# A delta-rule recurrence: rows kept in PSUM banks, and 16-wide diagonal blocks inverted elementwise on VectorE

## The reference

```
def step(state, inp):
    r_t, w_t, k_t, v_t, aa_t, bb_t = inp
    sa = jnp.einsum('bhvk,bhk->bhv', state, aa_t)
    state = state * w_t[:, :, None, :] + sa[..., None] * bb_t[:, :, None, :] + v_t[..., None] * k_t[:, :, None, :]
    return state, jnp.einsum('bhvk,bhk->bhv', state, r_t)
...
_, y = lax.scan(step, state0, (tm(r_h), tm(w_h), tm(k_h), tm(v_h), tm(-kk), tm(kk * a_h)))
```

## Time and profile before

| | us |
|---|---|
| median of three runs | 2084.86 (2081.75 to 2087.80) |
| the profiled execution, its own time | 2081.08 |
| its span in the trace | 2079.3 |
| TensorE busy | 2031.4 (98%) |
| VectorE busy | 1139.5 (55%) |
| GpSimd busy | 1178.7 (57%) |
| ScalarE busy | 536.0 (26%) |
| the recurrence, from the opening's D (1126.4) to the end of chain 6 (1565.9) | 439.5 |
| from one pair to the next in its middle | 61.4 |

### The profile page before, as it was taken

The page is one execution under the profiler, slowest core; times in us unless marked ns, Lnnn a source line. Parts: engine busy times, 40 slices in busy tenths (PEclk is TensorE's granted clock), DMA queues, the critical chain, the costliest instruction groups (busy, mean ns, idle before and its releaser), DMA issues.

```text
span 2079.3 us, 39898 instructions
## 1 busy us (share of the span) xinstructions
PE 2031.4 (98%) x16195; PEld 1678.5 (81%) x16195; DVE 1139.5 (55%) x1533; ACT 536.0 (26%) x1139; POOL 1178.7 (57%) x1175
## 2 busy tenths in 40 slices
PE   8999999999999999999999999999999999999998
PEld 6888888877877787788877888888886888888886
DVE  6878624466667654202068677666773655555312
ACT  2100002233434212313143133333223023333101
POOL 6888865634534475545547044433374867677764
PEclk9999999999999999999999999999999999999999
DMA  3323331353353422311323022111223432332231
GB/s 136 102 92 102 101 101 46 92 176 121 127 163 112 148 82 64 98 62 61 124 56 93 15 65 66 46 48 46 65 65 124 133 101 81 101 99 90 89 112 56
DMA packets 181243, 190.28 MB, mean 92 GB/s; under 512 B 8526, under 2 KB 162269, under 8 KB 180829
## 3 DMA queue, kind: packets, MB, share of 16 engines
q1 hardware_dynamic: 172288, 181.81, 27.6%
q10 hardware_dynamic: 8796, 6.21, 1.0%
HBM read 179.56 MB, written 8.44 MB: 90 GB/s over the span
## 4 chain that ended last, share of the span: by engine, by line
PE 61%; DVE 3%; issue 1%; POOL 1%; DVEq 1%; POOLq 1%; ACT 0%; ACTq 0%
PE bank L915 8%; PE bank L916 8%; PE bank L917 8%; PE bank L1592 7%; PE bank L1553 3%; PE bank L1405 3%; PE bank L1421 2%; PE bank L1423 2%; PE bank L1422 2%; PE bank L1690 2%; PE bank L1327 1%; PE bank L1328 1%; PE bank L1329 1%; PE bank L1080 1%; PE bank L1294 1%
## 5 line engine op out<-in xcount | busy, mean ns | idle before, releaser
L740 POOL TENSOR_SCALAR whi<-raws 128x1024 fp32r<-128x1024 f32 (+5 forms) x312 | 321.0, 1029 | 284.9 <-PE bank L1082 166.8
L746 POOL TENSOR_TENSOR wlo<-raws,whi 128x512 fp32r<-128x512 f32 (+5 forms) x312 | 400.8, 1285 | 0.0
L745 POOL TENSOR_TENSOR wlo<-raws,whi 128x512 fp32r<-128x512 f32 (+5 forms) x312 | 373.4, 1197 | 46.0 <-issue 3.0
L915 PE MATMUL bank<-hbuf,whi 128*128 128x512 f32 (+2 forms) x840 | 329.4, 392 | 1.8 <-POOL wlo L746 1.8
L917 PE MATMUL bank<-hbuf,wlo 128*128 128x512 f32 (+2 forms) x840 | 327.8, 390 | 0.0
L916 PE MATMUL bank<-hbuf,whi 128*128 128x512 f32 (+2 forms) x776 | 303.0, 390 | 0.0
L649 POOL TENSOR_TENSOR spare<-ones 1x1 f32<-1x1 f32 x92 | 21.4, 233 | 298.5 <-PE bank L917 208.2
L915 PEld LDWEIGHTS bank<-hbuf,whi 128*128 128x128 f32 (+2 forms) x840 | 157.1, 187 | 37.0 <-POOL wlo L746 3.1
L917 PEld LDWEIGHTS bank<-hbuf,wlo 128*128 128x128 f32 (+2 forms) x840 | 157.1, 187 | 34.1
L916 PEld LDWEIGHTS bank<-hbuf,whi 128*128 128x128 f32 (+2 forms) x776 | 145.2, 187 | 31.1
L672 POOL TENSOR_SCALAR lg2L<-lg 128x128 fp32r<-128x128 f32 x8 | 2.4, 298 | 221.7 <-DMA lg<-in_g 221.7
(11 more groups left out here) (544 smaller groups left out, 4747.1 us busy)
## 6 DMA issues: line engine op xcount, KB each, us to landing
adaw<-in_w_ada SPq DMA_DIRECT2D x64, 384.0 KB, 4.3
...
raws<-in_w_in SPq DMA_DIRECT2D x41, 512.0 KB, 3.9
...
```

The lines of the kernel that those rows point to most:

```text
L740: G.tensor_scalar(h_, r_, 1.0, 1.0, ALU.mult, ALU.mult)
L745: G.tensor_tensor(first[0], first[1], f32(first[2]), ALU.subtract)
L746: G.tensor_tensor(last[0], last[1], f32(last[2]), ALU.subtract).then_inc(raw_split, 1)
L915: M.matmul(dst, wh, acts[k][0], start=(first and k == 0), stop=False)
```

## The change

Three things are done together.

The 16 x 16 diagonal blocks of I - D are no longer inverted by products of all chunks. VectorE masks D and adds up the four blocks of a chunk column by column (`diagonal_blocks`). ScalarE's queue stores that to HBM in pieces of 64 bytes and loads it back so that each of 64 partitions holds the 256 numbers of one block (`blocks_gathered`; two heads x 8 chunks x 4 blocks are 64). VectorE inverts the blocks elementwise with broadcasts and reductions (`inverted_blocks`). Block and transpose go back through HBM (`blocks_kept`, `blocks_spread`) while the chain runs, after the copies of chunk 2 and of chunk 3 (one later in the first and the last chain), and VectorE spreads them with a mask (`spread_blocks`). `LEVELS` shrinks to four levels with five products. The product D moves out of the chain into the gates, behind their sixth product.

Some rows of the preparation (the norms of the keys, the direction of the keys, the changed key, the sums of the decays, the deviation of the result) live in PSUM banks 3, 4 and 5 instead of SBUF, and a few semaphores and waits follow.

VectorE's order changes: the pair two before is finished inside the preparation (`finished`), with the reciprocal and one multiply of it at the end of the part before (`deviations`), and the value rows are taken last. The first two preparations have an order of their own.

```diff
-    (("DA", "D", "N2"), ("D", "DA", "A2")),
-    (("N2", "A2", "A4"), ("A2", "U", "U")),
-    (("A4", "U", "V"),),
-    (("A4", "V", "V"),),
-    (("A4", "V", "V"),),
-    (("V", "I", "W"), ("E16", "V", "Z")),
+    (("E16", "V", "Z"),),
     (("W", "Z", "V"), ("Z", "W", "W")),
     (("E32", "V", "Z"),),
     (("W", "Z", "last"),),
 )
...
+BLK = 16
+BLOCKS_KEPT_AT = (3, 2, 2, 2, 2, 2, 3)
...
-GATE_BANK = ((0, 7), (4, 5), (0, 6))
+GATE_BANK = ((0, 7), (4, 5), (0, 7))
 GATE_ORDER = ((1, 0), (0, 1))
-GATES_BESIDE = {3: (0, 20), 6: (20, 34), 15: (34, 48)}
+GATES_BESIDE = {2: (0, 20), 5: (20, 34), 8: (34, 48)}
...
-LEVEL_BANK = ((1, 6),) * 7 + ((7,), (6,))
+LEVEL_BANK = ((1,), (1, 6), (7,), (6,))
+D_AFTER = 6
...
+        def deviation_tile(p):
+
+            return bank[4] if p < PAIRS - 1 else gn_dev
+
+        def decay_tiles(q):
+
+            return (lwd if q == 0 else bank[5], cc if q == 0 else bank[5], epos if q < 2 else bank[5])
...
             def gates(q):
 
                 pe.wait_ge(evac[0], fill("rkv", 0) + q + 1)
-                for n in range(3 * DT):
+                for n in range(D_AFTER):
                     gate_part(q, n)
-                pe.wait_ge(sem("rk.bonus"), q)
-                pe.wait_ge(sem("rk.y"), q)
+                gram(q, "D")
+                for n in range(D_AFTER, 3 * DT):
+                    gate_part(q, n)
+                pe.wait_ge(sem("rk.sig"), q + 1)
...
                 if name == "D":
-                    pe.wait_ge(sem("rk.kr"), q + 1)
+                    pe.wait_ge(sem("rk.ab"), q + 1)
...
+                    pe.wait_ge(sem("rk.kr"), q + 1)
                     pe.wait_ge(sem("rk.sig"), min(q + 1 + (q == 0), PAIRS))
                 elif name == "qb":
-                    pe.wait_ge(sem("rk.ge"), q * 8 + GRAM_TAKEN["E32"])
+                    pe.wait_ge(sem("rk.kr"), q + 1)
+                    pe.wait_ge(sem("rk.ge"), q * 5 + GRAM_TAKEN["E32"])
                 elif name == "qk":
...
+                chunk_products(bank[b], left, right).then_inc(sem("rk.block" if name == "D" else "rk.gram"), 1)
...
             def prepare(q, step):
 
                 if step == 1:
...
+                    gram(q, "A")
                 elif step == 2:
...
                     gram(q, "ak")
...
                 elif step == 6:
...
+                    gram(q, "qb")
+                elif step == 7:
+                    pe.wait_ge(sem("rk.ge"), q * 5 + GRAM_TAKEN["ak"])
                     turn(7, vT[q % 2], "rk.tv", centre)
...
                 elif step == 9:
...
+                    pe.wait_ge(sem("rk.ge"), q * 5 + GRAM_TAKEN["qb"])
+                    turn(0, kkT, "rk.tk")
                 elif step == 10:
...
                     pe.wait_ge(sem("rk.te"), q * 3 + 1)
                     turn(7, bT, "rk.tb")
                 elif step == 12:
+                    gram(q, "qk")
+                elif step == 14:
+                    level(q, 0, 0)
+                elif step == 16:
+                    level(q, 1, 0)
+                elif step == 17:
+                    level(q, 1, 1)
+                elif step == 19:
+                    level(q, 2, 0)
+                elif step == 21:
                     level(q, 3, 0)
...
-                pe.wait_ge(sem("rk.nr"), min(p + 2, PAIRS))
-                started(3, vtok, Gqk)
                 if p >= 1:
-                    pe.wait_ge(sem("gn.s"), p)
+                    pe.wait_ge(sem("gn.x"), p)
                 else:
                     pe.wait_ge(sem("gt.taken"), 4)
                 started(4, kN, vtok, hi=CHUNKS - 1)
+                pe.wait_ge(sem("rk.bon"), min(p + 2, PAIRS))
+                started(3, vtok, Gqk)
                 pe.wait_ge(sem("inv.dve"), (p + 1) * TAKEN_ALL)
+                pe.wait_ge(sem("rk.kr"), min(p + 2, PAIRS))
...
+            def blocks_gathered(q):
+
+                act.wait_ge(sem("blk.d"), q + 1)
+                act.dma_start(blocks_in[q % 2].rearrange("(c p j) -> p c j", c=CHUNKS, p=P),
+                              diagonal.rearrange("p (c j) -> p c j", c=CHUNKS)).then_inc(sem("blk.kept"), 16)
+                act.wait_ge(sem("blk.kept"), 16 * (q + 1))
+                act.dma_start(blk, blocks_in[q % 2].rearrange("(n x) -> n x", n=64)).then_inc(sem("blk.in"), 16)
+
+            def blocks_kept(q):
+
+                act.wait_ge(sem("blk.x"), q + 1)
+                act.dma_start(blocks_out[q % 2].rearrange("(w n x) -> n w x", w=2, n=64),
+                              hf[0:64, 0:2 * BLK * BLK].rearrange("n (w x) -> n w x", w=2)).then_inc(sem("blk.out"), 16)
+
+            def blocks_spread(q):
+
+                act.wait_ge(sem("blk.out"), 16 * (q + 1))
+                act.dma_start(hf[:, S + P:S + 3 * P].rearrange("p (x j) -> p x j", j=BLK),
+                              blocks_out[q % 2].rearrange("(x p j) -> p x j", p=P, j=BLK)).then_inc(sem("blk.back"), 16)
+
             def take_gates(q):
 
                 take_gate(q, 0)
+                if q >= 2:
+                    blocks_gathered(q)
                 take_gate(q, 1)
...
+                    if p + 1 < PAIRS and c == BLOCKS_KEPT_AT[p]:
+                        blocks_kept(p + 1)
+                    if p + 1 < PAIRS and c == BLOCKS_KEPT_AT[p] + 1:
+                        blocks_spread(p + 1)
...
-            take_gates(1)
+            blocks_gathered(0)
+            take_gate(1, 0)
+            blocks_kept(0)
+            blocks_spread(0)
+            take_gate(1, 1)
+            blocks_gathered(1)
...
+            def key_directions(q):
+
+                lengths = bank[3]
+                dve.wait_ge(sem("rk.nr"), q + 1)
+                V.reciprocal(lengths[:, :], lengths[:, :])
+                dve.drain()
+                V.scalar_tensor_tensor(lengths[:, :], Kr[:, :], pcol[q % 3][:, 5:6], lengths[:, :], ALU.mult, ALU.mult)
+                dve.drain()
+
+            def decayed_keys(q):
+
+                pc, par = pcol[q % 3], q % 2
+                direction = change = key = bank[3]
                 dve.wait_ge(sem("rk.sig"), q + 1)
...
                 dve.wait_ge(sem("rk.ex"), q + 1)
...
+                V.scalar_tensor_tensor(aT[par][:, :], direction[:, :], -1.0, lwd[:, :], ALU.mult, ALU.mult)
+                dve.drain()
+                V.tensor_tensor(direction[:, :], direction[:, :], cc[:, :], ALU.mult)
+                dve.drain()
+                V.tensor_tensor(bT[:, :], direction[:, :], aa[:, :], ALU.mult).then_inc(sem("rk.ab"), 1)
+                dve.drain()
+                V.tensor_scalar(change[:, :], aa[:, :], pc[:, 6:7], pc[:, 10:11], ALU.mult, ALU.add)
+                dve.drain()
+                V.tensor_tensor(key[:, :], Kr[:, :], change[:, :], ALU.mult)
+                dve.drain()
+                V.scalar_tensor_tensor(kkT[:, :], key[:, :], SCAN_SCALE, cc[:, :], ALU.mult, ALU.mult)
...
+            def deviations(p):
+
+                dev, pc = deviation_tile(p), pcol[p % 3]
+                dve.wait_ge(sem("gn.s"), p + 1)
+                V.reciprocal(dev[:, :], dev[:, :])
+                dve.drain()
+                V.scalar_tensor_tensor(gn_y[:, :], gn_y[:, :], pc[:, 8:9], dev[:, :], ALU.mult, ALU.mult)\
+                    .then_inc(sem("gn.x"), 1)
+                dve.drain()
+
             def finished(p):
 
-                x, pc = gn_x, pcol[p % 3]
-                dve.wait_ge(sem("gn.s"), p + 1)
-                V.reciprocal(gn_dev[:, :], gn_dev[:, :])
-                dve.drain()
-                V.scalar_tensor_tensor(x[:, :], gn_y[:, :], pc[:, 8:9], gn_dev[:, :], ALU.mult, ALU.mult)
-                dve.drain()
+                x, pc = gn_y, pcol[p % 3]
...
-                gram("D")
-                taken(inv_D, 1, "up16")
+                if q >= 2:
+                    inverted_blocks(q)
                 gram("A")
-                taken(inv_DA, 0, "low16")
-                dve.drain()
-                V.tensor_tensor(by_chunk(inv_U[:, :]), by_chunk(inv_D[:, :]),
-                                chunk_mask["id"][:, :].unsqueeze(1).to_broadcast([P, CHUNKS, CH]), ALU.add)\
-                    .then_inc(sem("rk.ge"), 1)
                 taken(inv_E16, 0, "step16")
                 taken(inv_E32, 0, "step32")
                 gram("ak")
                 taken(Gak, 7, "up1")
-                take_level(0)
-                take_turned(vtok, 7, "rk.tv")
                 if q == 0:
                     key_directions(1)
-                take_level(1)
+                if q < 2:
+                    inverted_blocks(q)
+                else:
+                    finished(q - 2)
                 gram("qb")
                 taken(Gqb[q % 2], 0, "up0")
-                take_level(2)
+                take_turned(vtok, 7, "rk.tv")
+                take_turned(kN, 0, "rk.tk")
                 take_turned(bN[q % 2], 7, "rk.tb")
-                take_level(3)
-                take_turned(kN, 0, "rk.tk")
-                take_level(4)
-                gram("qk")
-                taken(Gqk, 7, "up0")
```

(83 more changed lines are left out.)

167 lines of the change are left out of this document (77 added, 90 removed).

## The result

The changed kernel takes 2105.58 us (median of 4 runs, 2098.93 to 2110.96; the profiled one is the fastest of the four), beside 2086.05 us for the kernel before in the same comparison; the ratio is 1.0092, 95% interval 1.0072 to 1.0112. The forecast was 2069 us, so it is slower by 0.9% where 0.8% faster was forecast.

A forecast was written before the change was run, and what follows sets the result against it. TensorE was taken to bound the kernel: chains +23.0, gates -8.4, last preparation +0.9, opening +1.5 sum to 17 us won, rounded to 16, so 2081.1 becomes 2065 profiled and the median forecast is 2069; range 2060 to 2087.

The forecast's parts named there:

- slot prices: Chains: steps with full slots begin 1.17, 1.05 and 1.28 us apart; emptying a slot is worth 0.54 or 0.46 us.
- E32: Chain: a copy VectorE takes after its inversion, at +19.9, from the bank that slot 6's product overwrites.
- Wait: 0.2: Chain, slot 6: ready at +19.7, its product waits 0.2 us for VectorE's copies from its bank, at +19.9.
- the read back: Beside the gates' end: loading the blocks back from HBM takes 2.5 us, so they are there at +12.4.
- rival of the late blocks: Gates' end: weight loads delay the blocks by 1.8 us, giving 2078; 25% shared with a 9 us inversion on VectorE.
- The return: Chain: inverted blocks come back from HBM in 2,048 pieces within 2.9 us; slot 14 waits up to 0.3 us.
- D in the gates: Gates, after six products: this product waits 0.3 us for its input, and the gates end 1.4 us later.
- The clock: Chains: TensorE's granted clock falls in every chain, 9 us lost, 2078; chance 8%.
- one such fall stands before and after, so it cancels: Opening: TensorE's standstill brings one fall to the 1.2 GHz level, as in the kernel before, so no net cost.
- +0.9: Last preparation, chain 6: only 0.9 us won, from a load issued sooner within GpSimd's gapless run.
- here GpSimd is idle: VectorE's inversion: no GpSimd work beside it, so its time stays near the low end, 6.1 us (bounds 5.0 and 9).
- the chain begins 4.8 us earlier: Opening: preparation 0 gets shorter, so chain 0 begins 4.8 us earlier than at 1166.

## Why the prediction was wrong

*The chains.* The slot prices held in their sum. With E32 out of the way the five periods are 58.7 us on average, forecast 58.2; the kernel's own chain 5, without a fall, takes 59.46 with 1.4 us of wait. The step that failed is "Wait: 0.2" at slot 6. It was the difference of two large sums (19.9 against 19.7), each with an uncertainty of over 1 us: blocks 1.0 late, inversion 0.7 longer, against a slot 0.4 later. Two terms of the first sum were mis-sized: the read back, 3.8 us measured for 2.5, and the inversion, 6.8 for 6.1. The waits came to 8.3 us in five chains, and moving the copies won 11.9 us there, the falls included.

*The read back.* Forecast 2.5 us from small rows in other places; 3.7 to 4.5 in four of the five gates that have weight loads beside them and 2.6 in the fifth, 2.1 where there are none. This was the rival of the late blocks, priced at 1.8 us and given a share of 25%. The Trainium skill ("DMA: Bandwidth & Descriptors", section "Latency and other measured facts") has HBM latency at 0.2 us on average and 2 us under high load; by that rule the trace agrees in size, with 1.6 to 2.4 us between the loaded and the free read. No run here separates the latency of HBM from queueing behind the weight loads.

*The return.* Right: forecast 2.9, measured 2.9 where nothing is beside it, 3.8 at the most in chains 1 to 5, 0.4 to 0.7 us of wait in three of them. In chain 6 it took 5.5 us; there I had no step for it. The price of the Trainium skill ("DMA: Bandwidth & Descriptors", section "Anatomy of one DMA") that the prediction set beside it is fitted there to transfers that GpSimd issues, and ScalarE issues this one; by it the return would land in 2.3 us, an estimate, and no return landed in under 2.9.

*D in the gates.* Right: waits of 0.3 us on average (0.6 once), forecast 0.3; gates of 12.6 us, forecast 12.3.

*The clock.* Given 8% and named as an alternative, when it comes on top of whatever else goes wrong. It falls in the middle chains when slot 6 waits, not in them all, and in none of the kernels without that wait or with the slots before it filled. In the middle chains the empty slots alone so do not bring it about; which of the waiting chains is hit, no run settles. The three falls cost some 4 us in the middle, by the estimate above. In the opening it is 20.5 us long against 3.4, and my step "one such fall stands before and after, so it cancels" was wrong.

*Chain 6.* "+0.9" was the worst step. I had written that the small instructions are slow when GpSimd is beside them and that "here GpSimd is idle", and in the same text that GpSimd runs without a gap through chain 6. I used that run as a cover for TensorE's gain and never laid VectorE's inversion beside it. The stretch from chain 6 to chain 7 is 8.6 us longer than before the change, and chain 7 is 4.1 longer: 1.6 in a wait for `deviations`, which uses bank 4, and the rest at the lower clock. With GpSimd held back 3.4 of these 12.7 came back, with the inversion's arithmetic left out 9.5. The longest wait there, 6.2 us for the return, I had not priced.

*The opening and chain 0.* The step that failed is "the chain begins 4.8 us earlier": it began 3.4 us later after the opening's start, 8.2 us off, and chain 0 was longer than forecast by another 2.7. For chain 0 I had the pieces (the return for slot 14, 3.1 measured, 3.0 forecast; Gqb 2.7, forecast 2.3), but ScalarE's wait for the write costs 3.3 instead of 1.5. TensorE stood still for 12.2 us behind VectorE in this preparation (7.4 for the spread, 2.3 for Gqb, 2.5 in smaller waits), where I had 7; of the 7.4 the order on VectorE makes about 3. The lower clock covers 10.8 us of TensorE's busy time where it covered 3.4 before; at half speed that is some 3.7 us more, an estimate.

*PSUM rows.* The decay rows are worth nothing, as forecast; the others were not tried apart.

Together: 13.3 + 10.9 + 13.6 - 2.9, less 1 for the rounding of the sum, is the 34 us between the profiled execution that was forecast (2065) and the one measured (2098.9). Middle: the waits for E32 and the falls, 11.9 us together, are shown by experiment; how they divide is an estimate. Chain 6: it is shown that GpSimd's splits slow the inversion and so most of the wait for E32 there; why the return lands in 5.3 us even when issued earlier was not tried apart from the weight loads and splits beside it. Opening: the order's share is shown. Early blocks of pair 1 together with an early inverse won 0.4% (0.9992 to 0.9952) and shortened chain 0 (70.3 to 64.4 us); which of the two does it is not shown, and the clock's share was not separated.
